# Conditioning products of a hybrid decoder trunk: from split weights as the moving operand to unsplit fp32 weights as stationary blocks

## The chip, the cores and the metric

One core of one Trainium2 chip. The metric is the device time of one launch in microseconds (us), taken as the median of the runs; lower is better. The engines are named as the profile names them: PE (TensorE), PEld (its weight loads), DVE (VectorE), ACT (ScalarE), POOL (GpSimd) and SP (the engine whose queue issues most DMAs).

## The reference, cut to what matters

One layer on 1024 prompt tokens and 64 sample tokens (8 sequences of 8), 1088 in all, with d_model 1024. Nine conditioning vectors (one for the prompt, one for each sample sequence) give the modulation that all else depends on:

```python
sc = jax.nn.silu(c)                                             # 9 rows of 1024
mod = jnp.einsum('bd,de->be', sc, w_ada[l]) + b_ada[l]          # 1024 -> 6144
sh_m, sc_m, gt_m, sh_f, sc_f, gt_f = jnp.split(mod, 6, axis=-1)
h = rms_norm(x, g_mix[l]) * (1 + sc_m) + sh_m
u = jnp.einsum('btd,de->bte', h, w_in[l]) + b_in[l]             # 1024 -> 2048
...                                                             # conv of width 31, conv of width 4, RG-LRU
x = x + gt_m * (concat[A, B] @ w_out)
x = x + gt_f * (relu(h2 @ w_up)^2 @ w_down)                     # h2 modulated by sh_f, sc_f
```

All data is fp32. `w_ada` is 1024 x 6144, 24 MB: the largest weight beside `w_up` and `w_down` with 16 MB each. Of its output only 9 rows are wanted.

## The kernel before, in words

Every large product is made of three products of fp32r operands: a weight or activation is split in a high part (a copy rounded to fp32r, by ACT, or DVE for some activations) and a low part (original minus high part, by POOL or DVE), and high x high, high x low and low x high are summed in PSUM. In the code `strip` (L1466) is the product of one 128-column strip of a weight with one of three token chunks of 384, 384 and 320: 8 blocks of the contraction x 3 products, 24 matmuls.

The 6144 columns of `w_ada` are taken in 12 groups of 512. The token stage needs groups 0 to 3 (shift and scale of the mixer); groups 4 to 11 are needed after it.

- **Opening, groups 0 to 3.** SP loads them whole into `ada0` (2 MB each, in two halves by contraction block, rows of 2 KB), with tiles of x between them and the first two strips of `w_in` behind them. Groups 0 and 1 go through `ada_plain` (L1351): the 9 conditioning vectors, transposed (`c_t`), are the stationary operand of 9 columns and 512 fp32 weight columns move: 8 matmuls for a group. Groups 2 and 3 are split by ACT (`ada0_high`, L598) and DVE (`ada0_low`, L1051) and multiplied by `ada` (L1359) with `stk`, a stationary block that holds the conditioning's high part in columns 0 to 8 and its low part in columns 32 to 40: 16 matmuls of 512 columns for a group. Either way the result lies as rows; ACT copies it out (`rows9`, `group_rows`), PE turns it with four small fp32 matmuls (`turn9`, `group_turn0`), and ACT adds the bias into `mod` (`group_out`, L578).
- **Tokens.** ACT and DVE normalise the tiles of x (`norm_x`, `scale_x`). When groups 0 to 3 and the scale `sc_m` are in, 16 units of transposed tokens are modulated: `unit_full` on ACT (even units, L643) and on DVE (odd units, L1096), then split by both and POOL into `act_hi` and `act_lo`.
- **Steps 0 to 7** (`first_step` L1520, `step` L1497): each takes two strips of `w_in` (slots 0 and 1 of `w_hi`, `w_lo`), 6 strip products, 144 matmuls. ACT makes the high part of the next strip, POOL the low part (`strip_lo`, L369), and between them ACT evacuates, POOL multiplies by the gate (`product`, L387) and forms the samples' convolution terms (`sample_taps`), and DVE runs the width-31 convolution. In each step one of groups 4 to 11 goes along in four pieces (`ada_piece`, L1515): SP loads 512 KB (`load_ada`, L273, rows of 2 KB, two buffers), ACT splits (`ada_split`, L585), POOL splits (`split_ada`, L373), PE does four matmuls of 512 columns a piece. In the step after it the group's rows are turned by `group_turn` (L1368): four fp32 matmuls with the rows as stationary operand of 128 x 128 and 9 moving columns (`pick`). In step 1 these come right behind its first strip product, with the late pieces 2 and 3 of the group before. The loops of PE over steps 2 to 6 are hardware loops.
- **Behind the steps**: ACT squares the centred convolution (`squares`, L785, into `xsq`, a part of `tmp_b`); PE averages them (`var_a`, L1489); ACT takes roots (`deviation`). Then PE's `recurrent_gates(j)` (L1560), ACT's `recurrence(j)` (L806), POOL's square of a (L461) and DVE's `gated_input(j)` (L1204) run for j = 0 to 3, with five `turn_state` groups and their output DMAs between. POOL also spreads the sample gates over the tokens (`gt_tok`, L467, 16 copies). Then DVE has a chain of scans and splits, and then come the `w_out` product and the eight MLP blocks, in which PE is busy throughout.

Each engine runs its own instruction list in order and waits on semaphores; the order is written out by hand. The buffers overlay one another: the area of `raw_ada`, `aw_hi` and `ada_rows` is used for other things before and after.

Of the kernel before, what the change touches and what calls it, by code (L numbers as in the profile page):

```python
# [29 lines left out]
P = 128  # L30
D = 1024
# [35 lines left out]
ADA_PLAIN = 2  # L67
C_LO = 32
# [4 lines left out]
def trunk(nc, x_prompt, x_sample, c_prompt, c_sample, state_conv_a, state_conv_b, state_lru_h,  # L73
# [4 lines left out]
    with ctx:  # L78
# [17 lines left out]
        def sem(name):  # L96
# [9 lines left out]
        pick = sb("pick", [P, 9])  # L106
# [17 lines left out]
        rs = shared([("h_st", [9, WA], F32)], [("w_hi", [P, 2, D], F32R)])  # L124
        h_st, w_hi = rs["h_st"], rs["w_hi"]
        w_lo = sb("w_lo", [P, 2, D], F32R)
# [17 lines left out]
                     ("sg", [P, TOK], F32), ("ada_rows", [P, GW], F32),  # L144
                     ("tail_p", [P, J, KA - 1], F32)],
                    [("above_h", [P, J, TOK], F32), ("ada_h", [P, J, GA_W], F32R), ("ada_l", [P, J, RB_W], F32R)],
                    [("aw_hi", [P, 2, D], F32R), ("aw_lo", [P, 2, D], F32R)],
# [5 lines left out]
        ada_rows, aw_hi, aw_lo = rw["ada_rows"], rw["aw_hi"], rw["aw_lo"]  # L153
        ada_h, ada_l = rw["ada_h"][:, :, KA - 1:KA - 1 + D], rw["ada_l"][:, :, KB - 1:KB - 1 + D]
# [6 lines left out]
                    [("stage", [P, 4, WA], F32)], [("raw_ada", [P, 2, 2 * GW], F32)], [("xn", [P, 2, D], F32)])  # L161
        raw_ada = rt["raw_ada"]
# [8 lines left out]
        ada_in = [sem("ada_in0"), sem("ada_in1")]  # L171
# [4 lines left out]
        c_sig, c_silu, c_tr, c_cp = sem("c_sig"), sem("c_silu"), sem("c_tr"), sem("c_cp")  # L176
        par_tr, par_cp, sa_tr, sa_cp = sem("par_tr"), sem("par_cp"), sem("sa_tr"), sem("sa_cp")
        ada0_used, ada0_hi, ada0_lo, ada0_free = (sem(n) for n in ("ada0_used", "ada0_hi", "ada0_lo", "ada0_free"))
        ada_hi, ada_lo, ada_used = sem("ada_hi"), sem("ada_lo"), sem("ada_used")
        rows_out, ada_tr, ada_evac = sem("rows_out"), sem("ada_tr"), sem("ada_evac")  # L180
        c_zero = sem("c_zero")
# [46 lines left out]
        xsq = tmp_b[:, 0:J, :]  # L228
# [33 lines left out]
        def _(sp):  # L262
# [10 lines left out]
            def load_ada(m, i):  # L273

                wait(sp, ada_lo, 4 * m + i - 1)
                sp.dma_start(raw_ada[:, i % 2, :].rearrange("p (k n) -> p k n", n=GW),
                             wada_v[:, 2 * i:2 * i + 2, bass.ds(m * GW + ADA0 * GW, GW)]).then_inc(ada_in[i % 2], 16)

            sp.wait_ge(c_in, 32)
            for g in range(ADA0):  # L280
                for h in range(2):
                    sp.dma_start(ada0[:, g, 4 * h:4 * h + 4, :],
                                 wada_v[:, 4 * h:4 * h + 4, g * GW:(g + 1) * GW]).then_inc(ada0_in[g][h], 16)
# [5 lines left out]
            sp.wait_ge(nlo_even, KD + 1)  # L289
            sp.wait_ge(nlo_odd, KD)  # L290
            load_ada(0, 0)
            load_ada(0, 1)

            def step(m, nxt, apart=WA):

                if nxt is not None:
                    for s in range(2):
                        load_piece(2 * m + s + 1, s, win_v[:, :, bass.ds(nxt + s * apart, P)], True)
                load_ada(m, 2)
                load_ada(m, 3)  # L300
                if nxt is not None:
                    load_ada(m + 1, 0)
                    load_ada(m + 1, 1)

            with sp.Fori(0, J - 1) as j:
                step(j, (j + 1) * P)
            step(J - 1, 2 * WA, P)
            with sp.Fori(0, J - 1) as j:
                step(j + J, (j + 1) * (2 * P) + 2 * WA, P)
            step(2 * J - 1, None)  # L310
            for k in range(KD):
                load_piece(W_OUT0 + k - 1, k % 2, w_out[0, k * P:(k + 1) * P, :], False)
# [40 lines left out]
        def _(pool):  # L353
# [19 lines left out]
            def split_ada(q, slot):  # L373

                pool.wait_ge(ada_hi, q + 1)
                pool.tensor_tensor(aw_lo[:, slot, :], raw_ada[:, slot, :],  # L376
                                   aw_hi[:, slot, :].bitcast(F32), ALU.subtract).then_inc(ada_lo, 1)

# [27 lines left out]
            def step(m, glu, last):  # L406
                if not last:
                    strip_lo(2 * m + 2, 0, strip_a, NC * (m + 1))
                split_ada(4 * m + 2, 0)
                split_ada(4 * m + 3, 1)  # L410
                if not last:
                    strip_lo(2 * m + 3, 1, strip_b, NC * (m + 1))
                    split_ada(4 * m + 4, 0)
                if glu:
                    product(m)
                if not last:
                    split_ada(4 * m + 5, 1)
                if glu:
                    sample_taps(m, m % 2)

            split_ada(0, 0)
            split_ada(1, 1)
            product(0)
            strip_lo(2, 0, strip_a, NC)
            split_ada(2, 0)
            strip_lo(3, 1, strip_b, NC)
            split_ada(3, 1)
# [3 lines left out]
            split_ada(4, 0)  # L431
            split_ada(5, 1)
# [16 lines left out]
            step(2 * J - 1, False, True)  # L449
# [7 lines left out]
            pool.wait_ge(var_done, NC)  # L457
            for j in range(J):
# [3 lines left out]
                if j == 2:  # L462
                    pool.wait_ge(st_tr, 3)
                    pool.wait_ge(ada_evac, ADA_G)
                    for g, row0 in ((0, M_GTM), (1, M_GTF)):
                        for k in range(KD):
                            last = pool.tensor_copy(gt_tok[:, g, k, :].rearrange("p (b t) -> p b t", t=TB),  # L467
                                                    mod[:, row0 + k, 1:9].unsqueeze(2).broadcast_to([P, NB, TB]))
                    last.then_inc(tails, 1)
                    pool.wait_ge(ada_tr, ADA_G)  # L470
                    pool.wait_ge(st_tr, 1)
            pool.wait_ge(evac_a, 2 * J * NC)
            pool.wait_ge(evac_b, 2 * J * NC)
            for j in range(J):
# [4 lines left out]
                for k in ((), (4,), (5,), (6, 7))[j]:  # L479
                    w_out_lo(k)  # L480
            pool.wait_ge(lo_ready, W_OUT0 + KD)
# [23 lines left out]
        def _(act):  # L505
# [32 lines left out]
            act.wait_ge(c_silu, 1)  # L538
            act.wait_ge(c_zero, 1)
            act.activation(stk[:, :, 0:9], c_t[:, :, :], ACT.Copy).then_inc(c_cp, 1)  # L540

# [32 lines left out]
            def group_rows(g, bank):  # L574

                act.activation(ada_rows[:, :], ps[:, bank, :], ACT.Copy).then_inc(rows_out, 1)

            def group_out(g, bank, col):  # L578
                act.wait_ge(ada_tr, g + 1)
                for i in range(4):  # L580
                    last = act.activation(mod[:, bass.ds(4 * g + i, 1), :], ps[:, bank, col + 9 * i:col + 9 * i + 9].unsqueeze(1),
                                          ACT.Identity, bias=par[:, bass.ds(C_BADA + i + 4 * g, 1)])
                last.then_inc(ada_evac, 1)

            def ada_split(m, i):  # L585

                q, slot = 4 * m + i, i % 2
                wait_apart(act, ada_in[slot], 16 * (2 * m + i // 2 + 1))
                wait(act, ada_used, q - 1)
                act.activation(aw_hi[:, slot, :], raw_ada[:, slot, :],  # L590
                               ACT.Copy).then_inc(ada_hi, 1)

            def rows9(g):

                act.wait_ge(ada0_used, g + 1)
                act.activation(ada_rows[0:9, :], ps[0:9, 6 + g % 2, :], ACT.Copy).then_inc(rows_out, 1)

            def ada0_high(e):  # L598

                g, i = ADA_PLAIN + e // 4, e % 4  # L600
                act.wait_ge(ada0_in[g][i // 2], 16)
                wait(act, ada0_free, e - 3)
                act.activation(ada_h[:, e % 4, :], ada0[:, g, 2 * i:2 * i + 2, :].rearrange("p a b -> p (a b)"),
                               ACT.Copy).then_inc(ada0_hi, 1)

# [15 lines left out]
            rows9(0)  # L621
            for e in range(4):
                ada0_high(e)
            group_out(0, 0, P)
            norm_x(2)
            norm_x(3)
            rows9(1)
            for e in range(4, 8):
                ada0_high(e)
            group_out(1, 0, P + 36)  # L630
            norm_x(4)
            act.wait_ge(ada0_free, 4)
            group_rows(2, 6)
            strip_hi(0, 0, strip_a, 0)
            norm_x(5)
            group_out(2, 0, P + 72)
            act.wait_ge(ada0_free, 8)
            group_rows(3, 7)
            norm_x(6)
            group_out(3, 0, P + 108)  # L640
            act.wait_ge(sc_done, 1)

            def unit_full(u):  # L643
# [3 lines left out]
                wait(act, nlo_even, u // 2 - 1)  # L647
# [3 lines left out]
            def unit_high(u):  # L651

                k, cols, _ = unit(u)
                act.wait_ge(mf_d, u // 2 + 1)
# [3 lines left out]
            for p in range(KD):  # L658
                if p < KD - 1:
# [4 lines left out]
                if p == 1:  # L664
# [1060 lines left out]
```

## Time and profile before

| | us |
|---|---|
| median of 3 runs | 1296.06 |
| lowest, highest run | 1294.80, 4485.14 |
| the profiled execution's own time | 1296.5 |
| its span in the trace | 1294.7 |

One run of the three is far out; the other two and the profiled execution agree within 0.2%. A "record" is one entry of the profile: an fp32 matmul leaves two of them, a transpose and an fp32r matmul one. A record's length contains its way through the array, so the distance from start to start is what it costs. PEclk is the clock granted to TensorE: 1.00 is 2.4 GHz and 0.50 is 1.2 GHz.

### The profile page before, as it was taken

What the parts mean: (1) busy time and instruction counts of PE and PEld (TensorE: products, weight loads), DVE (VectorE), ACT (ScalarE), POOL (GpSimd) and SP (SyncE); (2) the same over time, 40 slices, a digit from 0 to 9 for tenths busy, and PEclk for the clock granted to TensorE, in tenths of its full rate; (3) what the DMA queues carried; (4) which work ended last, traced back from release to release, by engine and by line L of the source; (5) the groups of instructions that cost most, each with busy time, mean ns of one, the idle gap of its engine ahead of it and who ended that gap; (6) DMA issues with size and microseconds to landing.
All of it is one profiled execution on the core that took longest, in us unless ns stands there. A gap on an engine that the chain in (4) does not pass through costs nothing.

```text
span 1294.7 us, 16511 instructions
## 1 busy us (share of the span) xinstructions
PE 1192.5 (92%) x6175; PEld 1068.0 (82%) x6175; DVE 723.8 (56%) x809; ACT 402.8 (31%) x704; POOL 369.3 (29%) x217
## 2 busy tenths in 40 slices
PE   6798999999723999899999999999999999999996
PEld 2687999997423888888998998998988988988985
DVE  2649699996686455524534534535535435435447
ACT  4752334433791433420320320320310310311322
POOL 0246777652453010410320410410410311311300
PEclk9697999999966999899999999999999999999998
DMA  9533343321204110210210210310300300201102
GB/s 298 163 98 98 98 126 117 109 86 49 68 32 151 37 33 1 82 50 1 78 53 1 81 49 0 90 40 0 97 32 0 97 32 10 87 32 32 49 33 105
DMA packets 74661, 87.26 MB, mean 67 GB/s; under 512 B 3816, under 2 KB 53248, under 8 KB 74627
## 3 DMA queue, kind: packets, MB, share of 16 engines
q1 hardware_dynamic: 72448, 85.21, 21.1%
q10 hardware_dynamic: 2179, 1.61, 0.5%
q8 instruction: 20, 0.33, 0.1%
q14 instruction: 14, 0.11, 0.0%
HBM read 81.72 MB, written 5.08 MB: 67 GB/s over the span
## 4 chain that ended last, share of the span: by engine, by line
PE 85%; DVE 5%; SPq 2%; ACT 2%; POOL 2%; DMA 1%; issue 1%; ACTq 0%; DVEq 0%; POOLq 0%
PE ps L1472 15%; PE ps L1474 14%; PE ps L1473 14%; PE ps L1614 11%; PE ps L1615 11%; PE ps L1617 11%; PE ps L1480 1%; PE ps L1621 1%; PE ps L1620 1%; SPq L265 1%; PE ps L1365 1%; PE ps L1364 1%; DVE tmp_a L1235 1%; DMA x<-in_x_prompt 1%; DVE ga L1232 1%
## 5 line engine op out<-in xcount | busy, mean ns | idle before, releaser
L1472 PE MATMUL ps<-act_hi,w_hi 128*128 128x384 f32 (+1 forms) x1152 | 381.0, 331 | 8.0 <-DVE act_lo L1048 3.9
L1473 PE MATMUL ps<-act_lo,w_hi 128*128 128x384 f32 (+1 forms) x1152 | 378.4, 328 | 0.0
L1474 PE MATMUL ps<-act_hi,w_lo 128*128 128x384 f32 (+1 forms) x1152 | 378.3, 328 | 0.0
L1472 PEld LDWEIGHTS ps<-act_hi,w_hi 128*128 128x128 f32 x1152 | 218.7, 190 | 11.0 <-issue 4.8
L367 POOL TENSOR_TENSOR wb_lo<-raw,wb_hi 128x1024 fp32r<-128x1024 f32 x40 | 99.9, 2506 | 430.0 <-ACT wb_hi L568 403.3
L367 POOL TENSOR_TENSOR w_lo<-raw,w_hi 128x1024 fp32r<-128x1024 f32 x48 | 118.4, 2468 | 363.8 <-ACT w_hi L568 305.7
L1272 DVE TENSOR_TENSOR ps<-ps,gt_p 128x1024 f32<-128x1024 f32 x72 | 88.7, 1233 | 237.6 <-PE ps L1617 237.6
L1473 PEld LDWEIGHTS ps<-act_lo,w_hi 128*128 128x128 f32 x1152 | 218.8, 190 | 1.6
L1474 PEld LDWEIGHTS ps<-act_hi,w_lo 128*128 128x128 f32 x1152 | 218.6, 190 | 0.0
L1614 PE MATMUL ps<-wb_hi 128*128 128x512 f32 x512 | 199.4, 389 | 1.1 <-ACT gt_s L899 1.1
L1615 PE MATMUL ps<-wb_lo,wb_hi 128*128 128x512 f32 x512 | 199.2, 389 | 0.0
L1302 DVE TENSOR_TENSOR relu<-relu 128x384 f32<-128x384 f32 (+1 forms) x96 | 74.7, 778 | 199.3 <-ACT relu L942 199.3
L1617 PE MATMUL ps<-wb_hi,wb_lo 128*128 128x512 f32 x512 | 157.7, 389 | 0.0
L568 ACT ACTIVATE wb_hi<-raw 128x1024 fp32r<-128x1024 f32 x40 | 41.3, 1051 | 364.9 <-PE ps L1621 319.2
L1169 DVE SCALAR_TENSOR_TENSOR ps<-ga,caw,ps 128x1024 f32<-128x1024 f32 x112 | 134.2, 1282 | 0.0
L1614 PEld LDWEIGHTS ps<-wb_hi 128*128 128x128 f32 x512 | 96.1, 188 | 21.1 <-ACT gt_s L899 1.3
L1617 PEld LDWEIGHTS ps<-wb_hi,wb_lo 128*128 128x128 f32 x512 | 96.1, 188 | 20.0
L1615 PEld LDWEIGHTS ps<-wb_lo,wb_hi 128*128 128x128 f32 x512 | 96.1, 188 | 19.7
L942 ACT ACTIVATE relu<-ps 128x384 f32<-128x384 f32 (+1 forms) x96 | 45.2, 471 | 187.6 <-PE ps L1474 178.5
L1274 DVE TENSOR_TENSOR x<-x,ps 128x1024 f32<-128x1024 f32 x72 | 87.9, 1221 | 2.5
L1614 PE MATMUL ps<-wb_hi,act_hi 128*128 128x512 f32 x128 | 51.3, 401 | 39.9 <-DVE stk L1254 39.9
L376 POOL TENSOR_TENSOR aw_lo<-raw_ada,aw_hi 128x1024 fp32r<-128x1024 f32 x32 | 80.2, 2523 | 17.7 <-ACT aw_hi L590 17.7
(224 smaller groups left out, 1298.9 us busy)
## 6 DMA issues: line engine op xcount, KB each, us to landing
raw_ada<-in_w_ada SPq DMA_DIRECT2D x32, 512.0 KB, 3.7
raw<-in_w_up SPq DMA_DIRECT2D x32, 512.0 KB, 4.0
raw<-in_w_down SPq DMA_DIRECT2D x32, 512.0 KB, 3.3
ada<-in_w_ada SPq DMA_DIRECT2D x8, 1024.0 KB, 15.0
x<-in_x_prompt SPq DMA_DIRECT2D x16, 512.0 KB, 8.8
raw<-in_w_in SPq DMA_DIRECT2D x16, 512.0 KB, 4.8
raw<-in_w_out SPq DMA_DIRECT2D x8, 512.0 KB, 3.4
out<-x SPq DMA_DIRECT2D x8, 512.0 KB, 2.6
```

The source lines that it names most:

```text
L367: pool.tensor_tensor(dst, raw[:, slot, :], hi.bitcast(F32), ALU.subtract).then_inc(lo_ready, 1)
L376: pool.tensor_tensor(aw_lo[:, slot, :], raw_ada[:, slot, :], aw_hi[:, slot, :].bitcast(F32), ALU.subtract).then_inc(ada_lo, 1)
L1169: dve.scalar_tensor_tensor(out=out if k == KA - 1 else a, in0=win, scalar=w, in1=a, op0=ALU.mult, op1=ALU.add).then_inc(conva_tap, 1)
L1272: dve.tensor_tensor(src, src, gt_p[:, :], ALU.mult).then_inc(gated, 1)
L1274: dve.tensor_tensor(x2[:, t, :], x2[:, t, :], src, ALU.add).then_inc(rmw_done, 1)
L1302: dve.tensor_tensor(f, r, r, ALU.mult).then_inc(r2_done, 1)
L1472: mm(out, wh, xh, start=(k == 0), stop=False)
L1473: mm(out, wh, xl, start=False, stop=False)
L1474: last = mm(out, wl, xh, start=False, stop=(k == KD - 1))
L1614: mm(out, ah, wh, start=(k == 0), stop=False)
L1615: mm(out, ah, wl, start=False, stop=False)
L1617: last = mm(out, al, wh, start=False, stop=end)
```

## The change

All 12 groups are computed with the fp32 weights, not split, as the stationary operand: for each 128 output columns, 8 matmuls with a 128 x 128 block of `w_ada` stationary and the 9 columns of `c_t` moving, summed in PSUM. 32 fp32 matmuls (64 records) make a group, and the result is already laid out as `mod` wants it. DVE adds the bias in four instructions in all (`modulation`). Gone are `stk`'s conditioning part, `pick`, all of ACT's, POOL's and DVE's splits of `w_ada`, the row copies, the turns and `group_out`.

- Groups 0 to 3: `ada_first(g)`, at the places of `ada_plain` and, for 2 and 3, behind the state transposes; the loads are halved by output column (rows of 1 KB).
- Groups 4 to 10: group m+3 inside step m, m = 1 to 7, piece i behind a strip product of chunk 1 or 2; each piece has its own buffer (rows of 512 B), reloaded when its product is done.
- Group 11: behind `recurrent_gates(0)` and the first `turn_state`, from `ada_late`, which shares its place with `w_hi` and `w_lo` and so is loaded when the last strip is done.
- `unit_full` runs on ACT for all 16 units; norms of tiles 6 and 7 move behind its start. `xsq` lies on `lru`, so `squares(0)` moves ahead of the last evacuation but waits for the seventh group; the state transposes all use bank 6 and are spread over the gates; POOL's spread of the second gate moves behind the h_end copies; the step loops of PE and SP are written out.

```diff
-            def ada_plain(g):
-                for h in range(2):
-                    pe.wait_ge(ada0_in[g][h], 16)
-                    for k in range(4 * h, 4 * h + 4):
-                        last = mm(ps[0:9, 6 + g % 2, :], c_t[:, k, :], ada0[:, g, k, :], start=(k == 0), stop=(k == KD - 1))
+            def ada_first(g):
+                for i in range(4):
+                    if i % 2 == 0:
+                        pe.wait_ge(ada0_in[g][i // 2], 16)
+                    at = P + 36 * g + 9 * i
+                    for k in range(KD):
+                        last = mm(ps[:, 0, at:at + 9], ada0[:, g, k, i * P:(i + 1) * P], c_t[:, k, :],
+                                  start=(k == 0), stop=(k == KD - 1))
                 last.then_inc(ada0_used, 1)
...
+            def ada_piece(a, i):
+                w, done, n = (ada_step, ada_in, a + 1) if a < ADA_S else (ada_late, late_in, a - ADA_S + 1)
+                bank, at = 6 + a // 4, 36 * (a % 4) + 9 * i
+                pe.wait_ge(done[i], 16 * n)
+                for k in range(KD):
+                    last = mm(ps[:, bank, at:at + 9], w[:, i, k, :], c_t[:, k, :],
+                              start=(k == 0), stop=(k == KD - 1))
+                last.then_inc(ada_used, 1)
...
-            def step(m, last=False, late=()):
+            def step(m, last=False, group=None):
...
                         strip(s, (s + c) % 2, c, done)
-                        if c == 0 and s == 0:
-                            for i in late:
-                                ada_piece(m - 1, i)
-                            group_turn(m + ADA0 - 1, 7, 0)
-                        for i in ((), (2 * s,), (2 * s + 1,))[c]:
-                            ada_piece(m, i)
+                        if group is not None and c > 0:
+                            ada_piece(group, 2 * s + c - 1)
...
-            step(1, late=(2, 3))
-            with pe.Fori(2, 2 * J - 1) as m:
-                step(m)
-            step(2 * J - 1, True)
-            group_turn(ADA_G - 1, 7, 0)
+            for m in range(1, 2 * J - 1):
+                step(m, group=m - 1)
+            step(2 * J - 1, True, ADA_S - 1)
...
             pe.wait_ge(tails, 1)
+            recurrent_gates(0)
             turn_state(0, 6, KA - 1, lambda j: tail_p[:, j, :])
-            turn_state(1, 7, 4 * (KA - 1), lambda j: tail_a[:, j, 0:120])
-            recurrent_gates(0)
+            late_group(ADA_S)
+            turn_state(1, 6, 4 * (KA - 1), lambda j: tail_a[:, j, 0:120])
+            recurrent_gates(1)
...
+            def modulation(first, last, src):
+                b = par[:, C_BADA + first:C_BADA + last].unsqueeze(2).broadcast_to([P, last - first, 9])
+                dve.tensor_tensor(mod[:, first:last, :], src.rearrange("p (r c) -> p r c", c=9), b,
+                                  ALU.add).then_inc(ada_evac, 1)
...
+            dve.wait_ge(ada0_used, ADA0)
+            modulation(0, 16, ps[:, 0, P:P + 144])
```

## Rows read from the trace of the kernel before

**Rows 1.** The page: engines, granted clock in 40 slices, chain that ended last.
```profile
PE 1192.5 (92%) x6175; PEld 1068.0 (82%) x6175; DVE 723.8 (56%) x809; ACT 402.8 (31%) x704; POOL 369.3 (29%) x217
...
PEclk9697999999966999899999999999999999999998
...
PE 85%; DVE 5%; SPq 2%; ACT 2%; POOL 2%; DMA 1%; issue 1%; ACTq 0%; DVEq 0%; POOLq 0%
```

**Rows 2.** Windows by stage: stretch, length, busy (instructions), PEclk, DMA share, GB/s.
```profile
8.60:52.07 43.47, 36.15 (x129) 19.38 (x130) 20.00 (x43) 28.98 (x59) 2.39 (x1) 0.86 0.95 310
66.61:92.50 25.89, 25.89 (x161) 25.62 (x162) 13.04 (x30) 11.32 (x19) 10.46 (x6) 0.99 0.33 97
98.21:138.94 40.73, 35.57 (x177) 33.89 (x178) 38.17 (x32) 9.71 (x19) 25.02 (x16) 0.83 0.40 117
138.94:167.31 28.37, 28.37 (x170) 27.67 (x169) 19.63 (x16) 10.51 (x20) 23.41 (x16) 1.00 0.35 99
280.81:316.50 35.69, 35.69 (x193) 32.00 (x191) 30.29 (x26) 9.52 (x18) 16.29 (x10) 1.00 0.18 60
320.72:331.87 11.15, 10.53 (x25) 5.89 (x25) 5.00 (x3) 6.36 (x8) 0.48 (x1) 0.73 0.00 0
331.87:367.24 35.37, 23.97 (x94) 15.95 (x95) 22.34 (x12) 31.53 (x37) 24.32 (x24) 0.91 0.25 77
367.24:408.23 40.99, 1.14 (x8) 0.93 (x7) 39.87 (x41) 24.10 (x32) 19.00 (x12) 0.54 0.08 26
```

**Rows 3.** Line 1356, groups 0 and 1: record length ns min/median/max, first and last start us.
```profile
L1356 PE MATMUL ps<-ada,c_t x32: 592/592/1057, 8.6 to 26.1; 128*9 128x512 f32 x32
```

**Rows 4.** Windows of PE alone: stretch, length, busy (records), PEclk, DMA share, GB/s.
```profile
111.35:113.05 1.70, 1.70 (x8) 0.50 0.27 67
113.05:118.50 5.45, 5.45 (x18) 0.50 0.47 139
47.00:50.20 3.20, 1.86 (x12) 1.00 0.22 50
50.30:51.80 1.50, 0.60 (x4) 0.50 0.00 0
344.00:357.00 13.00, 8.16 (x24) 1.00 0.28 86
```

**Rows 5.** Timeline of DVE, last scaled prompt tile before the first strip.
```profile
60.87 0.75 DVE L1020 TENSOR_SCALAR x<-x,ssq 128x1024 f32<-128x1024 f32 x1
```

**Rows 6.** Timeline of POOL between the first two steps.
```profile
95.61 2.38 POOL L367 TENSOR_TENSOR w_lo<-raw,w_hi 128x1024 fp32r<-128x1024 f32 x1
```

**Rows 7.** Timeline of PE in steps 1 to 3: single records, x8 merged.
```profile
137.98 0.39 PE L1364 MATMUL ps<-aw_hi,stk 128*128 128x512 f32 x1
...
138.91 0.34 PE L1472 MATMUL ps<-act_hi,w_hi 128*128 128x384 f32 x1
...
171.47 0.95 PE L1372 MATMUL ps<-pick,ada_rows 128*128 128x9 f32 x8
172.28 0.43 PE L1472 MATMUL ps<-act_hi,w_hi 128*128 128x384 f32 x1
172.55 0.34 PE L1473 MATMUL ps<-act_lo,w_hi 128*128 128x384 f32 x1
```

**Rows 8.** DMA issues of the page: KB each, us to landing.
```profile
raw_ada<-in_w_ada SPq DMA_DIRECT2D x32, 512.0 KB, 3.7
...
raw<-in_w_in SPq DMA_DIRECT2D x16, 512.0 KB, 4.8
```

**Rows 9.** Timeline of ACT behind the last step.
```profile
319.08 4.03 ACT L789 ACTIVATE tmp_b<-conv_a 128x1536 f32<-128x1536 f32 x3
```

**Rows 10.** Timelines of ACT, POOL and DVE in the recurrent stage.
```profile
343.08 0.90 ACT L800 ACTIVATE tmp_a<-ps,hb 128x768 f32<-128x768 f32 x1 [0.38 <-ACT stage L817]
...
355.54 5.04 POOL L467 COPY gt_tok<-mod 128x64 f32<-128x64 f32 x16
...
365.92 1.29 DVE L1211 SCALAR_TENSOR_TENSOR tmp_a<-tmp_b,tmp_a 128x1088 f32<-128x1088 f32 x1 [1.89 <-POOL tmp_b L461]
```

More of the change, by code:

```diff
@@ L170, in trunk @@
         gf_in, stored = sem("gf_in"), sem("stored")
-        ada_in = [sem("ada_in0"), sem("ada_in1")]
+        ada_in = [sem(f"ada_in{i}") for i in range(4)]
+        late_in = [sem(f"late_in{i}") for i in range(4)]
         staged_out = sem("staged_out")
@@ L288, in _, with load_out @@
                     load_x(t)
[L289 to L296, printed above, removed]
-                    for s in range(2):
[L298 to L311, printed above, removed]
-                load_piece(W_OUT0 + k - 1, k % 2, w_out[0, k * P:(k + 1) * P, :], False)
+            sp.wait_ge(c_tr, 1)
+            sp.wait_ge(par_tr, 1)
+            sp.wait_ge(sa_tr, 2)
+            for i in range(4):
+                load_ada(0, i)
+            for m in range(2 * J):
+                if m < 2 * J - 1:
+                    nxt, apart = ((m + 1) * P, WA) if m < J - 1 else (2 * WA + (m + 1 - J) * 2 * P, P)
+                    for s in range(2):
+                        load_piece(2 * m + s + 1, s, win_v[:, :, nxt + s * apart:nxt + s * apart + P], True)
+                if 0 < m < ADA_S:
+                    for i in range(4):
+                        load_ada(m, i)
+            def load_out(k):
+                load_piece(W_OUT0 + k - 1, k % 2, w_out[0, k * P:(k + 1) * P, :], False)
+            load_out(0)
+            load_out(1)
+            sp.wait_ge(strip_a, 2 * J * NC)
+            sp.wait_ge(strip_b, 2 * J * NC)
+            for a in range(ADA_S, ADA_G - ADA0):
+                for i in range(4):
+                    load_ada(a, i)
+            for k in range(2, KD):
+                load_out(k)
             sp.wait_ge(yhi_done, J)
@@ L463, in _ @@
                     pool.wait_ge(st_tr, 3)
[L464 to L471, printed above, removed]
+                    pool.wait_ge(ada_evac, 2)
+                    sample_gate(0, M_GTM)
             pool.wait_ge(evac_a, 2 * J * NC)
@@ L572, in strip_hi @@
                 hi(n, slot, w_hi[:, slot, :], 16 * (n // 2 + 1))
[L574 to L604, printed above, removed]
             def norm_x(t):
@@ L695, in gelu_out, with step @@
                           par[:, bass.ds(C_BIN + 3 * J + j, 1)], done)
-            def step(m, first, last, out_a, out_b):
-                if not first:
-                    wait_apart(act, ada_used, 4 * m)
-                    group_rows(m + ADA0 - 1, 6)
+            def step(m, last, out_a, out_b):
                 for c in range(NC):
-                    if c == 2 and not first:
-                        wait_apart(act, ada_tr, m + ADA0)
-                        group_out(m + ADA0 - 1, 7, 0)
                     wait_apart(act, strip_a, NC * m + c + 1)
@@ L765, in out_a, with out_b @@
                     gelu_out(c, bank, 2 * q, evac_a)
-                step(q + J + J // 2, False, last, out_a,
-                     lambda c, bank: gelu_out(c, bank, 2 * q + 1, evac_b))
+                def out_b(c, bank):
+                    if last and c == 2:
+                        squares(0)
+                    gelu_out(c, bank, 2 * q + 1, evac_b)
+                step(q + J + J // 2, last, out_a, out_b)
             with act.Fori(1, J) as j:
@@ L1078, in _ @@
             dve.tensor_scalar(hb[:, 1, :], par[:, C_BGX:C_BGX + J], 0.5, None, ALU.mult).then_inc(k_done, 2)
-            for e in range(4):
-                ada0_low(e)
             for h in range(2):
@@ L1568, in recurrent_gates, with late_group @@
                            start=True, stop=True).then_inc(done, 1)
+            def late_group(a):
+                for i in range(4):
+                    ada_piece(a, i)
             for c in range(NC):
```

290 lines of the change are left out of this document (87 added, 203 removed).

## The prediction

> **What bounds the kernel now.** I read the page first. PE is busy for 92% of the span and holds 85% of the chain that ended last; its clock is at the higher level in all but some slices, and the exceptions lie in the first tenth and around slice 11 [rows 1]. So a change pays only in what it gives to or takes from PE's path, or in the stages where PE waits. The second view, windows by stage [rows 2], says which is which. To 52.07 us the conditioning of groups 0 to 3 is made and everything waits for it. From there to 66.61 is the modulation chain of ACT, DVE and POOL; from 66.61 to 92.50 step 0, PE busy for all 25.89 us. Step 1 takes 40.73 us with PE busy for 35.57, while step 2 takes 28.37 with PE busy for all of it, and steps 3 to 6 repeat this. Step 7 with its means takes 35.69, all PE. Behind it ACT and PE alternate in the variances (11.15 us), ACT is the fullest in the recurrent stage (31.53 of 35.37 us), and DVE has the 40.99 us before `w_out` almost to itself. Behind 408.23 nothing is touched that PE waits for.
>
> **The price of the new product.** The trace of before has it: `group_turn` is an fp32 matmul with 128 x 128 stationary and 9 moving columns, two records. At 2.4 GHz eight records start at 171.47, the next strip product at 172.28, and the one behind that 0.27 later where two products at this level lie 0.17 apart; the insertion costs 0.81 + 0.09 = 0.90 us for eight, or 0.112 a record [rows 7]. At 1.2 GHz eight records fill 1.70 us, 0.213 a record [rows 4]. Each is paced by its weight load, not by 9 columns: a group is 64 records, 7.2 us at the high level and 13.6 at the low one. The Trainium skill (TensorE: Matmul & The Clock Gate, section LDWEIGHTS) gives a load about one 1.2 GHz cycle for each column, 107 ns, with no mention of the clock level; the first row is close to it, the second is twice it, so the rows decide. By the page's figure alone the opening would come out as in the first rival below.
>
> **Which level.** In the opening the new products are all that PE does. In 111.35 to 113.05 PE was full of them and stayed at 0.50, and the strips behind them, PE full again, still ran at 0.50 to 118.50. In 47.00 to 50.20, where such records were part of 1.86 us of work, the clock was still 1.00 and from 50.30 it was 0.50 [rows 4]. The opening of before begins at the low level too (line 1356's records are 1057 ns long at first and 592 later [rows 3]), and what raised it there, products of 512 moving columns, is gone. I take 1.2 GHz for the whole opening.
>
> **The sum, part by part.**
> 1. *Opening.* Group 0 can start at 8.6, when its load is there [rows 3]. Group 0 13.7 to 22.3, parameter transposes 1.2, group 1 to 37.2, state transposes 1.6, group 2 to 52.5, sixteen token transposes at 0.213 each 3.4, group 3 to 69.6 us (transposes estimated at the same 0.213). Loads are hidden: the DMA share is 0.95 and all of them are in by 52.07 as before [rows 2]. Bias and scale on DVE 0.8: 70.4 against 52.07. **+18.3.** If that cover were gone (loads in 1 KB rows slower by a tenth) the DMAs would still be done 20 us before PE.
> 2. *Modulation chain.* ACT has all 16 `unit_full` (0.7 each, was 9) and the norms of tiles 6 and 7 in it. Unit 8 needs tile 7 scaled; that ended at 60.87 + 0.75 = 61.6, 9.5 behind the start of the chain [rows 5]. In the new order I count on ACT 3 units and a split, a strip's high part, 2 units, a split, a norm, a wait for POOL, 2 units, a split, a norm: 10.6, then 0.9 on DVE, 11.4. The last transposes follow. **+1.9**; bounds -1 (chain hidden) and +5 (all seven extra units bare).
> 3. *Steps 0 and 1.* Step 0 is unchanged, and so is the way over POOL into step 1 (product, then the strip's low part at 95.61, 2.38 us [rows 6]). Step 1 loses its stall: the late pieces waited for POOL and the turn for ACT. It becomes 144 strip matmuls and four pieces. A steady step is 28.37; four pieces of four matmuls are 4 x 0.93 (137.98 to 138.91) = 3.72 and the turn 0.90 [rows 7], so the strips are 23.75. A piece of 16 records is 16 x 0.112 = 1.79, a group 7.2. Step 1 = 23.75 + 7.2 = 30.9, plus 2.5 for starting at 1.2 GHz behind the 5.7 us gap (bounds 1.7 and 5): 33.4 against 40.73. **-7.3.**
> 4. *Steps 2 to 6.* 7.2 instead of 4.6: **+12.8** for five. ACT's and POOL's splits that go were not on the path (10.51 and 23.41 us busy of 28.37 [rows 2]): worth nothing. Loads now come as 512 B rows; the `w_in` strips already do, with 4.8 us to landing against 3.7 [rows 8]; four of them have some 28 us. SP's `w_in` loads now stand behind a wait for the step's last piece, but still land 14 us before ACT wants them.
> 5. *Step 7 to the first variance.* 35.69 - 4.6 + 7.2 = 38.3, then `squares(0)` waits for the last piece, 1.34 (4.03 for three [rows 9]) and handovers: 39.8, where before it was 39.9 from 280.81 to 320.72. **-0.1.** The variances start behind some 3.4 us of narrow work and waiting, as they did at a PEclk of 0.73 [rows 2]: **-0.4**, bounds -3.5 (high level) and +2.
> 6. *Recurrent stage.* The late group stands before `recurrent_gates(1)`. Its load (2 MB) is in by then. It begins at the high level and falls: some 32 records at 0.112 and 32 at 0.213, 10.4 us. ACT's `recurrence(1)`, which started 11.8 behind the end of the variances (343.08 [rows 10]), starts at 18.3; the staging copies and high parts that stood before it partly fill the hole, and half of the `gt_tok` copies leave POOL's path (5.04 for 16 [rows 10]). I get the last `gated_input` done 40.9 instead of 36.0 behind the variances (365.92 + 1.29 [rows 10]), with 0.3 for the new bias instruction. **+4.9**, bounds +2 (all at the high level) and +8 (all at the low). Then the same 41 us of DVE.
>
> Sum: 18.3 + 1.9 - 7.3 + 12.8 - 0.1 - 0.4 + 4.9 = +30.1. On the profiled execution's own 1296.5 that is 1326.6; it stands 0.4 above the median, so I predict 1326.
>
> **Rivals.**
> - *The narrow products hold the high clock* (or a load costs the same at both levels). Then group 0 ends at 15.8, the parameters hold PE until 19.6, group 1 ends at 26.8, group 2, whose loads come at 28 and 31, at 35.4, and with the transposes group 3 at 44.4 (load times estimated from the share of the queue moved by then). The opening ends at 45.2, 6.9 before the old one instead of 18.3 behind it, 25 us less than my sum; with the late group and the variances at the high level as well, 1293 to 1301: not slower. It decides if eight records take 0.9 us there and not 1.7. For it: at 143 and 171 they do. Against: [rows 4]. The Trainium skill (same page, The HAM clock gate) says that matmul work lifts the throttle; if that held for these products alone, this rival would come true. The trace does not agree: 111.35 to 113.05 was full of them at 0.50. 8%.
> - *The pieces pull the clock down inside the steps.* A piece is 1.8 us of narrow work beside strips. Against: in 344 to 357 PE was busy for 8.16 of 13.00 us and stayed at 1.00; for: the fall at 50.3 with 1.86 of 3.20 busy, a good part narrow [rows 4]. The price of a fall is what strips lose from 113.05 on, 18 in 5.45 us where 31 fit at 0.173: 2.3 us. If 10 to 18 of the 28 pieces cost that, it is +23 to +41: 1350 to 1367. 16%.
> - *A wait I hold for covered comes to the surface*, in the steps above all: the written-out loops of PE, or SP's queue behind the last piece. Against it: "issue" holds 1% of the chain, and SP's queue 2% [rows 1]. It is in the upper part of my range.
>
> **How the numbers follow.** My sum 76%, itself from 1316 to 1336 by its bounds; the high clock 8%; falling clock in steps 16%. 2% of 1296, 25.9 us, is about what a measurement of this kernel can tell from no change; the line is at 1322. A quarter of the first case lies below it (0.20), and most of the second: same 0.24. Slower: the rest of the first and all of the third, 0.72. Faster by over 2% would need the second case and a gain of 20 us more: 0.04. Range 1310 to 1350.
>
> **What would show it.** `sc_m` written at 70, not 52 or 45; PEclk 0.50 over the opening with records 0.213 apart; step 1 near 33 us and steps 2 to 6 at 30.9 with PEclk 1.00; no ACT or POOL work on `w_ada`; gates(1) some 6 us later behind the variances. I am wrong if the opening runs at 1.00, if the step period is not 30.9, or if the stage from 331.87 on, moved by the sum, changes by more than 8 us.

## The result, and the profile after

The changed kernel takes 1323.51 us (median of 4 runs, 1323.43 to 1326.26) against 1296.48: ratio 1.0218, 95% interval 1.0198 to 1.0238. Slower, by 27.0 us, where 1326 was predicted; the interval lies clear of no change, but its lower end is just under the 2% that the prediction drew as its line, so whether the change costs more than 2% is not settled. The four runs of the kernel before still hold the one at 4485.14; the other three are 1294.80 to 1296.90. Its profiled execution took 1323.47 with a span of 1321.7.

The page of the kernel after: engines, granted clock, chain; it answers [rows 1].

```profile
PE 1234.0 (93%) x6655; PEld 1132.2 (86%) x6655; DVE 694.6 (53%) x794; ACT 355.5 (27%) x611; POOL 293.6 (22%) x185
...
PEclk9868999999875899999999999999999999999998
...
PE 91%; DVE 5%; ACT 3%; issue 1%; DMA 1%; POOL 0%; ACTq 0%; DVEq 0%; POOLq 0%
```

PE has 41.5 us more of work and is 91% of the chain instead of 85%: SP's queue and POOL have left it, while ACT holds 3% where it held 2%. The new products put more on PE's path than those waits had cost. Over the whole span ACT (-47.3) and POOL (-75.7) are emptier, and that is worth nothing in itself.

Windows by stage of the kernel after; they answer [rows 2].

```profile
0.00:52.05 52.05, 44.71 (x215) 44.30 (x216) 9.25 (x27) 16.65 (x28) 4.45 (x12) 1.00 0.99 322
52.05:66.78 14.73, 14.17 (x82) 14.10 (x83) 0.55 (x3) 0.01 (x1) 0.00 (x0) 0.73 0.18 53
66.78:84.42 17.64, 8.79 (x40) 8.09 (x40) 10.66 (x20) 14.58 (x24) 8.83 (x6) 0.50 0.11 30
84.42:116.50 32.08, 26.42 (x162) 25.91 (x161) 10.65 (x26) 13.23 (x23) 10.48 (x8) 0.93 0.01 1
116.50:149.30 32.80, 32.80 (x210) 32.80 (x211) 32.80 (x28) 5.57 (x10) 11.08 (x10) 0.94 0.28 80
149.30:180.10 30.80, 30.80 (x210) 30.80 (x209) 30.09 (x25) 5.57 (x10) 14.03 (x13) 1.00 0.37 103
...
303.50:343.11 39.61, 37.86 (x232) 35.05 (x231) 15.51 (x20) 4.63 (x8) 2.98 (x6) 0.99 0.17 56
343.11:353.60 10.49, 10.38 (x24) 5.79 (x24) 4.35 (x3) 5.46 (x8) 0.00 (x0) 0.73 0.47 142
353.60:394.80 41.20, 30.31 (x134) 22.27 (x135) 21.50 (x16) 31.36 (x38) 21.18 (x16) 0.81 0.21 66
394.80:435.66 40.86, 6.13 (x32) 5.69 (x31) 39.89 (x39) 25.69 (x34) 24.63 (x20) 0.54 0.08 26
```

Some bounds of these windows lie a few tenths behind the first product of their stage; by the first products, as in the table below, the stages are as follows. Everything ahead of the first strip is longer (66.61 us before, 84.42 now). Step 1 (116.50 to 149.01) takes 32.5 where it took 40.7. Steps 2 to 6 (to 303.08) are 30.8 each instead of 28.4. From the end of the variances (354.11) to DVE's first product with `m_t` (394.84), it is 40.7 where it was 35.8, and from there to `w_out` 40.8 where it was 40.5. The 1.00 of the first window is not the level there; the pace of the records tells it, and the last section says why.

Where the 1.2 GHz stretches lie, in the timeline of PE over the opening and in two windows of line 1251 alone (records in brackets):

```profile
8.33 13.79 PE L1251 MATMUL ps<-c_t,ada 128*128 128x9 f32 x64 [4.02 <-DMA ada<-in_w_ada]
...
23.21 13.82 PE L1251 MATMUL ps<-c_t,ada 128*128 128x9 f32 x64
...
38.52 13.68 PE L1251 MATMUL ps<-c_t,ada 128*128 128x9 f32 x64
52.05 3.51 PE L1286 MATMUL ps<-ident,x 128*128 128x128 f32 x16
55.39 10.66 PE L1251 MATMUL ps<-c_t,ada 128*128 128x9 f32 x64
```

```profile
55.30:58.50 3.20, 3.11 (x29) 3.20 (x29) 1.00 0.00 0
59.00:62.40 3.40, 3.40 (x18) 3.40 (x17) 0.50 0.00 0
```

Groups 0 to 2 take 13.7 to 13.8 us each, 0.213 a record as predicted. Group 3 takes 10.66: behind sixteen transposes with 128 moving columns the clock was granted at 1.00 for a few microseconds (29 records in 3.20 us), and with nothing but 9-column products in it fell back to 0.50 (18 in 3.40) though PE was full in both windows. Five of the six profiled executions with this opening (this one and runs 2, 3, 4 and 7) show such a rise, with group 3 at 10.6 to 10.9 us; in run 6 it didn't come.

| part of the sum | predicted | measured | from |
|---|---|---|---|
| opening, to `sc_m` | +18.3 | +14.7 | 52.07 to 66.78 |
| chain to the first strip | +1.9 | +3.1 | 14.54 to 17.64 |
| step 0 and the way into step 1 | 0 | +0.4 | 31.64 to 32.08 |
| step 1 | -7.3 | -8.1 | 40.66 to 32.51 |
| steps 2 to 6 | +12.8 | +12.2 | 141.86 to 154.07 |
| step 7 to the first variance | -0.1 | +0.1 | 39.95 to 40.03 |
| variances | -0.4 | -0.2 | their ends move 22.2 |
| recurrent stage | +4.9 | +4.9 | DVE's first product with `m_t` moves 27.1 |
| to `w_out` and behind | 0 | -0.1 | `w_out` moves 27.4, the span 27.0 |
| sum | +30.1 | +27.0 | |

### The profile page after: what moved, and what is told of

The parts are those of the page before. It is cut to its first block, busy times and chain, and to the rows that moved or that the text cites. A ratio compares the mean times of both kernels' runs of the same rounds, so it can differ in the third digit from the quotient of the medians.

```text
span 1321.7 us, 16976 instructions
## 1 busy us (share of the span) xinstructions
PE 1234.0 (93%) x6655; PEld 1132.2 (86%) x6655; DVE 694.6 (53%) x794; ACT 355.5 (27%) x611; POOL 293.6 (22%) x185
## 4 chain that ended last, share of the span: by engine, by line
PE 91%; DVE 5%; ACT 3%; issue 1%; DMA 1%; POOL 0%; ACTq 0%; DVEq 0%; POOLq 0%
PE ps L1328 14%; PE ps L1330 14%; PE ps L1329 14%; PE ps L1460 11%; PE ps L1463 11%; PE ps L1461 11%; PE ps L1261 4%; PE ps L1251 4%; PE ps L1336 1%; PE ps L1467 1%; PE ps L1466 1%; DVE tmp_a L1128 1%; DVE ga L1125 1%; PE ps L1286 1%; PE ps L1406 1%
## 5 line engine op out<-in xcount | busy, mean ns | idle before, releaser
L1460 PEld LDWEIGHTS ps<-wb_hi,act_hi 128*128 128x128 f32 x128 | 24.7, 193 | 39.9 <-issue 34.9
## 6 DMA issues: line engine op xcount, KB each, us to landing
ada<-in_w_ada SPq DMA_DIRECT2D x8, 1024.0 KB, 12.2
```

Of the source, the lines that this page charges most:

```text
L1460: mm(out, ah, wh, start=(k == 0), stop=False)
```

## The experiments

The theory: the sum stands, and its largest term is the clock, which stays low because 9 moving columns are all that PE does. The first rival is that the stationary form has one pace of its own in that stage; others are given with each run. All runs start from the kernel after, and a time is a median of four against seven runs of the kernel before taken beside them (median 1295.88, for runs 9 and 10 1295.12). "Less" and "more" are against the 1323.51 of the kernel after, which was not run again beside them.

**1. More columns in the opening.**

```diff
-  mm(ps[:, 0, at:at + 9], ada0[:, g, k, ...], c_t[:, k, :], ...)
+  mm(ps[:, 0, at:at + 126], ada0[:, g, k, ...],
+     c_t[:, k, :].unsqueeze(1).broadcast_to([P, 14, 9]), ...)
```

> The same products in the opening, but with 126 moving columns instead of 9 (the nine repeated 14 times; the surplus is overwritten by the next block). Theory, the low clock makes the opening long: with more columns the clock is granted 1.0 early, records come 0.112 us apart instead of 0.213, and scale_m is written near 46 to 50 us instead of 66.8; the run takes 1303 to 1308 us, 16 to 20 less than 1323.5. Rival, the weight load has one pace of its own in this stage, whatever the clock: the clock may rise, but records stay 0.21 apart and the time stays within 2 us of 1323.5. Second rival, the columns themselves cost: at the low level 126 columns take longer than the load, and the opening grows beyond 67.

1301.51 us, 22.0 less (ratio to before 1.0044, 1.0027 to 1.0060). Timeline of PE in this run:

```profile
8.31 9.68 PE L1251 MATMUL ps<-c_t,ada 128*128 128x126 f32 x64 [4.02 <-DMA ada<-in_w_ada]
...
18.67 7.41 PE L1251 MATMUL ps<-c_t,ada 128*128 128x126 f32 x64
...
27.95 7.41 PE L1251 MATMUL ps<-c_t,ada 128*128 128x126 f32 x64 [1.04 <-DMA ada<-in_w_ada]
...
36.94 7.31 PE L1251 MATMUL ps<-c_t,ada 128*128 128x126 f32 x64
```

The same 64 weight loads go through in 7.4 us instead of 13.8, and all records now carry 14 times the columns. Only the first third of group 0 is slow: 20 records in the first 3.7 us, 15 in the next 2.0. `sc_m` is written at 44.9, near the 45.2 that the prediction's first rival had for a high clock. The first strip comes 21.8 earlier (62.61), and that is what the whole run gained. The rival of one pace is out. Nothing but the number of columns was changed, and with it these instructions got the clock that halves their cost. My expectation of 16 to 20 was too small, as it took the end to be at 46 to 50.

**2. The norms ahead of the chain.** ACT first, then DVE, whose `scale_x(4)` to `scale_x(8)` go from behind the conditioning's bias to ahead of it.

```diff
-            norm_x(4)
-            norm_x(5)
+            for t in range(4, NT):
+                norm_x(t)
             act.wait_ge(sc_done, 1)
...
-            scale_x(3)
+            for t in range(3, NT):
+                scale_x(t)
             dve.wait_ge(par_cp, 4)
```

> The norms of tiles 4 to 8 (ACT) and their scaling (DVE) all stand ahead of the modulation chain, in the time in which ACT waits for the conditioning. Theory, the chain from scale_m to the first strip is set by ACT's order, two norms in it: 17.6 us become 14 to 15, the run 1320 to 1321, 2.5 to 3.5 less. Rival, the chain is set by PE's transposes or by the scale and bias instructions themselves: no more than 1 us goes.

1320.29 us, 3.2 less (1.0193, 1.0176 to 1.0210). First modulated unit on ACT and first strip on PE:

```profile
66.76 2.12 ACT L579 ACTIVATE xn<-ps,mod,sc_m 128x512 f32<-128x512 f32 x3 [17.04 <-DVE sc_m L916]
```

```profile
79.57 0.41 PE L1321 MATMUL ps<-act_hi,w_hi 128*128 128x384 f32 x1 [1.47 <-issue]
```

66.76 to 79.57 is 12.8 us where it was 17.64. In the kernel after ACT's norms stand inside, each with a scaling on DVE behind it:

```profile
72.09 1.07 ACT L524 ACTIVATE sg<-x 128x1024 f32<-128x1024 f32 x1
...
77.53 1.04 ACT L524 ACTIVATE sg<-x 128x1024 f32<-128x1024 f32 x1
```

The profiled execution gained 5.0 at `w_out`, the median 3.2. So the norms inside the chain had set its length, and by more than I expected (14 to 15). The run moves ACT's norms and DVE's scalings together and doesn't tell the two apart.

**3. The late group behind all gates.**

```diff
             turn_state(0, 6, ...)
-            late_group(ADA_S)
...
             turn_state(4, 6, ...)
+            late_group(ADA_S)
```

DVE's `modulation(44, 48)` goes behind its second scan.

> The late group (64 records, 9.9 us) stands behind the last gate products and state transposes instead of between the first and second, and its bias addition behind DVE's second scan. Theory, it delayed ACT's recurrence(1) and all behind it: the run takes 1318 to 1319.5, 4 to 5.5 less. Rival, ACT and DVE were late for another reason in that stage (the staging copies, POOL's squares): no more than 1.5 us goes. It would be slower if DVE's addition waits for the pieces beside the scans.

1317.83 us, 5.7 less (1.0179, 1.0161 to 1.0198), a little above the expected 4 to 5.5. In the kernel after, the group on PE and the second recurrence on ACT:

```profile
358.30 9.86 PE L1261 MATMUL ps<-c_t,ada_late 128*128 128x9 f32 x64
```

```profile
371.76 0.90 ACT L709 ACTIVATE tmp_a<-ps,hb 128x768 f32<-128x768 f32 x1 [2.02 <-PE ps L1406]
```

In this run:

```profile
365.35 0.90 ACT L709 ACTIVATE tmp_a<-ps,hb 128x768 f32<-128x768 f32 x1 [2.02 <-PE ps L1407]
```

```profile
379.77 9.88 PE L1262 MATMUL ps<-c_t,ada_late 128*128 128x9 f32 x64
...
429.26 0.76 PE L1461 MATMUL ps<-wb_hi,act_hi 128*128 128x512 f32 x1 [23.48 <-DVE stk L1148]
```

ACT's `recurrence(1)` starts at 365.35 instead of 371.76. Of these 6.4 us, 1.4 were there before the stage began (the first gate product is at 352.74 instead of 354.11), where nothing was edited. From the first gate product to `w_out` it is 76.5 us instead of 81.6, 5.0 less, and that is the prediction's term of +4.9. At 379.77 the group costs nothing: PE waits for DVE both behind it and again before `w_out`.

**4. Every piece in the steps twice.** `ada_again` is the 8 matmuls of a piece into the same columns.

```diff
                         if group is not None and c > 0:
+                            ada_again(group, 2 * s + c - 1)
                             ada_piece(group, 2 * s + c - 1)
```

> Each of the 28 pieces in steps 1 to 7 is computed twice. Theory, a piece costs its weight loads, 16 records of 0.112 us, and nothing hides it: 28 times 1.75 is 49 us more, 1372 to 1374, with the clock still 1.0 in the steps. Rival, the narrow stretches pull the clock down once they are 3.4 us long: beyond 1380, with PEclk below 1 in the steps. Second rival, a part of a piece hides a wait of PE: less than 44 us more.

1407.41 us, 83.9 more (1.0860, 1.0842 to 1.0878). The first rival. Window of the steps in this run:

```profile
120.00:280.00 160.00, 160.00 (x995) 160.00 (x993) 143.33 (x118) 20.46 (x37) 47.83 (x42) 0.86 0.24 68
```

PE is full and the clock is at a mean of 0.86. With single pieces, in the kernel after, it is 1.00 from 120 to 340. 49 of the 84 us are the products at their price at the high clock; the other 35 go with the lower clock, which run 6 tests. The prediction's second rival is a real mechanism, though the change as it is doesn't set it off.

**5. The moving form in the opening.** ACT copies the rows to `arow`, and 16 transposes at the end turn them.

```diff
-  last = mm(ps[:, 0, at:at + 9], ada0[:, g, k, i * P:(i + 1) * P], c_t[:, k, :], ...)
+  last = mm(ps[0:9, 6 + g % 2, :], c_t[:, k, :], ada0[:, g, k, :], ...)
```

> The four opening groups with the weights as moving operand (512 columns, 9 outputs), rows copied by ACT and turned at the end, all else as in the kernel after. Theory, what the opening lost is the clock: these products raise it, scale_m is written at 46 to 51 us, the run takes 1303 to 1308 us, 16 to 21 less than 1323.5; that is no better than the wide stationary form (1301.5), as both are then held by the loads. Rival, the stationary form itself, not the clock, is what is faster or slower: then this run differs from the wide one by over 8 us.

1305.95 us, 17.6 less (1.0081, 1.0064 to 1.0098), 4.4 above run 1. The first two groups on PE, and the writing of `sc_m` on DVE:

```profile
11.22 9.86 PE L1260 MATMUL ps<-ada,c_t 128*9 128x512 f32 x16 [6.93 <-DMA ada<-in_w_ada]
...
22.12 7.03 PE L1260 MATMUL ps<-ada,c_t 128*9 128x512 f32 x16 [0.26 <-DMA ada<-in_w_ada]
```

```profile
L928 DVE SCALAR_TENSOR_TENSOR sc_m<-mod,par x1: 232/232/232, 47.5 to 47.5; 128x72 f32<-128x72 f32 x1
```

Once the clock is high a group costs 7.03 in this form and 7.4 in the wide stationary one: the form doesn't decide, the clock does. `sc_m` comes 2.8 later than in run 1, for the late start (PE waits for both halves, 11.22 against 8.31) and the copies and turns at the end. Another 1.5 is lost behind it: ACT still has the norms of tiles 4 and 5 to do behind its last row copy, and its first modulated unit starts at 49.20.

**6. Every piece twice, all with 126 columns.** In `ada_again` and `ada_piece`:

```diff
-  mm(ps[:, bank, at:at + 9], w[:, i, k, :], c_t[:, k, :], ...)
+  mm(ps[:, bank, at:at + 126], w[:, i, k, :],
+     c_t[:, k, :].unsqueeze(1).broadcast_to([P, 14, 9]), ...)
```

> As the run with every piece computed twice, but all products of a piece with 126 moving columns; opening as in the kernel after. Theory, the clock fell there because 9 columns are little work: with 126 it stays at 1.00 in steps 1 to 7, a piece keeps its load price, and the run takes 1370 to 1376 us (1323.5 + 49). Rival, it fell because fp32 records stood too long between the strips, whatever their width: 1400 to 1412 as with 9 columns. Second rival, 126 columns take longer than the load even at the high level: over 1412.

1368.02 us (1.0556, 1.0538 to 1.0574), 39.4 less than run 4 with the same number of instructions. Window of the steps, and group 3 of the opening, whose products are those of the kernel after:

```profile
120.00:280.00 160.00, 160.00 (x1130) 160.00 (x1129) 153.44 (x126) 22.88 (x41) 55.62 (x52) 0.99 0.30 86
```

```profile
55.47 13.66 PE L1251 MATMUL ps<-c_t,ada 128*128 128x9 f32 x64
```

The mean clock of the window is 0.99, and it was 1.00 from 160 on. From the first strip to the first variance this run takes 308.2 us against 258.7, 49.5 for 28 pieces of 16 records: 0.110 a record, with 126 columns as with 9. A piece has no cover at all. The median lies 2 below the expected range, since the wide pieces also kept the clock high through the variances and the late group (85.2 us from the variances to `w_out`, 92.6 in the kernel after). The second fence is chance, as the opening is the same as in the kernel after: in this execution the short rise in group 3 didn't come, the group took 13.66 and `sc_m` was written at 69.9, within 0.5 of the predicted 70.4.

**7. Four groups in PE's idle stage.** Groups 8 to 11, 9 columns each, write bank 3 and get their bias ahead of `scales(sc_f)`; `w_out`'s second tile waits for it. SP's loads of rows of `w_out` stand between those of the groups.

```diff
-ADA_S = 7
+ADA_S = 4
...
-            late_group(ADA_S)
...
             gates(M_GTM, 4, 6)
+            for a in range(ADA_S, ADA_G - ADA0):
+                late_group(a)
```

> Groups 8 to 11 all behind the gate products of M_GTM, in the 35 us in which PE waits for w_out's operands, 9 columns each; steps 5 to 7 hold no group. Out of the steps go 3 x 7.2 = 21.6, out of the recurrent stage 5.7. Theory, the narrow products run at 1.2 GHz there: 4 x 13.7 = 55 us from 395 on end at 450, 20 past the start of w_out (430): 1323.5 - 21.6 - 5.7 + 20 = 1316, range 1311 to 1320. Rival, they run at the high level: 29 us, nothing past it, 1296 to 1298.

1306.36 us, 17.2 less (1.0090, 1.0072 to 1.0107), better than I expected. The four groups and the first `w_out` product on PE, and a window of the groups alone:

```profile
367.88 50.50 PE L1263 MATMUL ps<-c_t,ada_late 128*128 128x9 f32 x256
418.23 0.77 PE L1464 MATMUL ps<-wb_hi,act_hi 128*128 128x512 f32 x1
```

```profile
375.00:395.00 20.00, 20.00 (x96) 20.00 (x95) 0.50 0.68 205
```

The mechanism is the expected one: mostly 0.50, 96 records in 20 us, and `w_out` starts the moment the last piece is through. Of my 10 us too many, 4.5 are the groups themselves (50.5 us and not 55: they began at the high level, 42 records in the first 4.6 us). Another 2.8 is that I gave PE 35 us for them, where run 8 shows 37.8 from the end of the gate products to `w_out`'s operands. Some 2 us stay unexplained.

**8. The parts together.** The edits of runs 1, 2 and 7, and in the late pieces:

```diff
-  mm(ps[:, 3, at:at + 9], w[:, i, k, :], c_t[:, k, :], ...)
+  mm(ps[:, 3, at:at + 126], w[:, i, k, :],
+     c_t[:, k, :].unsqueeze(1).broadcast_to([P, 14, 9]), ...)
```

> The wide opening, the norms ahead of the chain, and groups 8 to 11 behind the gate products of M_GTM with 126 columns. Theory: each part is worth what it was alone and they add: 1301.5 - 3.2 - 5.7 - 21.6 = 1271, range 1267 to 1275, with w_out's first products at 1.00 from the start; 2% below the kernel before. Rival, four groups with 126 columns don't fit before w_out (a piece waits for its reload): 1275 to 1285. Second rival, the norms' gain is gone once the opening is short, since ACT and DVE have no time for them: 3 us more.

1276.11 us (0.9843, 0.9827 to 0.9860): faster than before, but 5 above the sum and just outside my range. DVE at the end of the opening, and the end of the late groups on PE:

```profile
50.35 0.74 DVE L928 TENSOR_SCALAR x<-x,ssq 64x1024 f32<-64x1024 f32 x1
51.02 0.29 DVE L914 TENSOR_TENSOR mod<-ps,par 128x144 f32<-128x144 f32 x1
```

```profile
349.36 14.56 PE L1257 MATMUL ps<-c_t,ada_late 128*128 128x126 f32 x128
365.49 14.98 PE L1257 MATMUL ps<-c_t,ada_late 128*128 128x126 f32 x128 [1.58 <-DMA ada_late<-in_w_ada]
387.16 0.76 PE L1458 MATMUL ps<-wb_hi,act_hi 128*128 128x512 f32 x1 [6.68 <-issue]
```

The late groups fit, and the way from the first strip to `w_out` is 322.7 (351.4 in run 1). But PE waits 6.68 us for `w_out`'s operands, and the first product there is not at 1.00 as I expected: its record is 0.76 long, as in the kernel after. The second rival came true as well: with the opening at 45 the norms ahead are no longer free. ACT waited until 47.3 for a tile's load, DVE scaled tile 8 at 50.35 and only then added the bias, so `sc_m` came at 51.6 instead of 44.9 and the first strip at 64.45 instead of 62.61.

**9. One norm ahead, bias first.** Run 8 without the edit of run 2, and on ACT (DVE's scalings follow):

```diff
             norm_x(5)
+            norm_x(6)
             act.wait_ge(sc_done, 1)
...
-                if p in (1, 2, 4):
-                    norm_x((6, 7, 7, 8)[p - 1])
+                if p in (0, 4):
+                    norm_x((7, 8)[p // 4])
```

> As the run with all parts together, but only the norm of tile 6 ahead of the chain, that of tile 7 behind the first split, and the conditioning's bias before the scaling of tiles 4 to 8. Theory, all norms ahead cost there what they had gained before: DVE's bias addition stood behind tile 8, whose load came at 49, and scale_m at 51.3 instead of 44.7. Then scale_m is back at 44.9, the first strip starts at 59 to 61 instead of 64.5, and the run takes 1270 to 1273 us, 3 to 6 less than 1276.1. Rival, the chain is held by units that wait for POOL's and DVE's low parts, whatever the norms: first strip at 62.6 as in the wide opening alone, and 1273.5 to 1275.

1271.22 us (0.9820, 0.9803 to 0.9836). First strip, first product of step 1, first product of `w_out`, three timelines of PE:

```profile
60.06 0.41 PE L1334 MATMUL ps<-act_hi,w_hi 128*128 128x384 f32 x1 [2.15 <-issue]
...
91.34 0.66 PE L1334 MATMUL ps<-act_hi,w_hi 128*128 128x384 f32 x1 [5.64 <-POOL w_lo L370]
...
381.31 0.77 PE L1467 MATMUL ps<-wb_hi,act_hi 128*128 128x512 f32 x1 [4.64 <-issue]
```

As expected: `sc_m` is written at 44.6 again, and the first strip starts at 60.06, 2.5 ahead of run 1. The rival (62.6) is out.

**10. Five late groups.**

```diff
-ADA_S = 4
+ADA_S = 3
...
-            modulation(16, 32, ps[:, 6, 0:144])
+            modulation(16, 28, ps[:, 6, 0:108])
```

> As the one before, and group 7 too behind the gate products (five groups there, three in steps 1 to 3). Theory, PE had 6.7 us left before w_out and a group takes 7.4 with 1.6 of waiting: the steps give back 7.2, w_out starts about 1 to 2 late: 5 to 6.5 us less than with four. Rival, the reloads of the fifth group stand in SP's queue behind a w_out row block that is loaded late: nothing or a loss.

1267.20 us (0.9781, 0.9758 to 0.9803), 4.0 less than with four, short of the 5 to 6.5 that I expected. Three timelines of PE, step 0, step 1 and the end of the late groups:

```profile
60.51 0.66 PE L1334 MATMUL ps<-act_hi,w_hi 128*128 128x384 f32 x1 [2.62 <-issue]
...
94.55 0.66 PE L1334 MATMUL ps<-act_hi,w_hi 128*128 128x384 f32 x1 [5.67 <-POOL w_lo L370]
...
366.78 14.56 PE L1266 MATMUL ps<-c_t,ada_late 128*128 128x126 f32 x128 [1.08 <-DMA ada_late<-in_w_ada]
381.09 0.48 PE L1467 MATMUL ps<-wb_hi,act_hi 128*128 128x512 f32 x1
```

`w_out` starts at 381.09, no earlier than the 381.31 of run 9. Two things took up the 7.2 us that the steps gave back. The fifth group fills PE to the end. And step 0 took 34.0 us instead of 31.3: its first 5.5 us ran at 0.50 here (17 records) and at 1.00 in run 9's profiled execution (41 records in 5.9 us). Nothing was edited there, so I take that as chance between executions; with an equal start the profiled executions would differ by some 6.5 us and not 3.7 (an estimate: 3.7 + 2.8), within what I expected.

The gain lies behind `w_out`'s start. PE comes to it at the high clock, with no wait ahead of it: 16 records in the first 2.9 us against 6 in the first 2.7, and the span behind that point is 883.5 instead of 887.0. This version beats both kernels, by 2.2% (0.2 to either side) and 4.3%.

## Why the prediction was right, and where its sizes were off

- *Opening.* The step held: 1.2 GHz and 0.213 a record, shown as the cause by run 1, which changes nothing but the number of columns. The term was 3.6 too large in the profiled execution, since "1.2 GHz for the whole opening" was false for half of group 3; in run 6's execution of the same opening it was 0.5 too large. The fastest and the slowest of the four runs of the kernel after differ by 2.8. The slowest has a mean granted clock of 0.969 where the others have 0.959, and run 6's profiled execution, without the rise, has 0.977 where two of its other runs have 0.967. So the slowest probably lacked the rise; only one of the four is profiled. That the total came within 3 us is no luck of errors that cancel: the opening is the only term off by more than 1.2.
- *The price of a weight load.* The rows show 0.110 to 0.113 us a record at 2.4 GHz and 0.213 at 1.2 GHz. The Trainium skill (TensorE: Matmul & The Clock Gate, section LDWEIGHTS) gives a load's time as its columns over 1.2, for 128 columns 107 ns, with no clock level: within a few per cent at the high one, half the measured price at the low one.
- *The level of the clock.* PE full of 9-column products fell to 0.50 in group 3, and in run 7's late groups it fell and stayed there, while in run 6 the doubled pieces with 126 columns kept 0.99 where those with 9 had 0.86. The Trainium skill (same page, The HAM clock gate) says that activity releases the throttle; by that rule the opening would have run at 1.00, and the trace does not agree: PE was never idle in these stretches. The rival of a high clock had 8%; run 1 is the kernel in which its condition holds, and took 1301.5, just above its 1293 to 1301, with the late group still narrow.
- *Chain.* Mis-sized by 1.2: +3.1. I counted 11.4 us to the last scaling of tile 7 and a constant rest; the scaling came at 79.2, 12.4 behind the start.
- *Steps.* 7.2 a group, no cover, and step 1's stall gone: -8.1 and +12.2 against -7.3 and +12.8. The falling clock (16%) didn't come; with double pieces it did (run 4). Its 35 us lie within the +23 to +41 that I had priced it at, but that price was for 10 to 18 falls by single pieces, so the agreement proves little.
- *Recurrent stage.* +4.9 as worked out: `recurrence(1)` started 18.3 us behind the variances, and by run 3 (5.0 us) the place of the group is the whole of it.
- *Left open.* Why the clock rises in group 3 in most executions and not in all, and why step 0 starts at the high clock in some. No run was made for either.

## What to carry to other kernels

Here a weight-stationary fp32 product cost its weight load, with 9 moving columns as with 126, and the load cost nearly double at 1.2 GHz (0.213 us a record against 0.110 to 0.113). Further columns were free up to 126, the most that was tried. So try to widen a thin product that runs alone, and read the pace of its records before and after. Then look at where a product stands before looking at what it costs: the same groups that cost 7.2 us each inside PE-bound steps cost nothing in the stage where PE waits for DVE, as long as they fit into it (run 7's narrow ones did not quite). And when a stage gets shorter, price again what had been hidden in it, as the norms in run 8 show.

## What the runs showed of the hardware that was not expected

- Records of the same products with 9 and with 126 moving columns follow each other 0.11 us apart at 2.4 GHz: 117 more columns cost nothing.
- The narrow pieces left the clock in the steps at 1.00, the same pieces doubled brought its mean to 0.86, and doubled with 126 columns it was 0.99.
- The clock column of a window prints 1.00 for the first 52 us of the kernel after, where records are 0.213 us apart. In run 7 this pace stands beside 0.50, and from 358.30 to 362.30 in the late group of the kernel after 37 records in 4 us stand beside 1.00. In run 6's profiled execution, where group 3 had no rise, the column prints 1.00 up to 87 us. So it can't be used ahead of its first change in these traces, and the pace of records of known form can.
